# Attention: chunk outputs turned by plain transposes, halves added by VectorE, inverse of the sums applied in the output block by GpSimd

## The reference, cut to what matters

```python
p = jax.nn.softmax(jnp.where(mask, s, -jnp.inf), axis=-1)      # fox heads; the memory heads without a mask
o = jnp.einsum('bhqk,bkhd->bqhd', p.astype(v.dtype), v)
...
y = jnp.concatenate([_normalize(y_conv), _normalize(y_fox), _normalize(y_mem)], axis=-1)   # RMS norm of each group
y = (y * out_norm_g).astype(y_conv.dtype)
return y @ w_out
```

## Time and profile before

| | |
|---|---|
| median of 3 runs | 2729.73 us (2722.56 to 2731.79) |
| span of the profiled execution | 2721.6 us |
| PE, DVE, POOL, ACT busy | 96%, 72%, 64%, 43% |
| attend, 560 to 1116 us: PE, POOL, DVE, ACT busy | 519.9, 536.7, 475.7, 427.0 us of 556 |

### The profile page before, as it was taken

How to read it: one execution, slowest core, us unless ns; L and a number is a source line. 1 busy time by engine, 2 the same in 40 slices (tenths; PEclk the granted TensorE clock), 3 DMA queues, 4 the chain that set the end, 5 groups by cost and what they waited for, 6 DMA issues and landing times. The chain is left out here.

```text
span 2721.6 us, 42356 instructions
## 1 busy us (share of the span) xinstructions
PE 2611.8 (96%) x14722; PEld 2358.1 (87%) x14722; DVE 1950.3 (72%) x2561; ACT 1168.6 (43%) x2053; POOL 1733.3 (64%) x1004
## 2 busy tenths in 40 slices
PE   8999999889999998899999999999999999999998
PEld 7999899877777777777799998999999997888887
DVE  5366687588888888666587888787887784454564
ACT  4222321377777778533353334333433332232343
POOL 3487688489999999565656776677656660222232
PEclk9999999999999999999999999999999999999999
DMA  6587899666667676775635343534345536755564
GB/s 207 176 258 251 272 295 308 174 175 177 174 187 192 181 191 185 232 247 188 201 105 174 115 132 114 174 114 132 115 117 152 157 104 202 245 171 179 182 227 139
DMA packets 470965, 498.20 MB, mean 183 GB/s; under 512 B 172171, under 2 KB 359558, under 8 KB 469722
## 3 DMA queue, kind: packets, MB, share of 16 engines
q1 hardware_dynamic: 449970, 470.00, 57.5%
q10 hardware_dynamic: 20496, 24.45, 2.6%
q0 software_dynamic: 288, 1.05, 0.1%
HBM read 398.11 MB, written 94.16 MB: 181 GB/s over the span
## 5 line engine op out<-in xcount | busy, mean ns | idle before, releaser
L2792 PE MATMUL ps_gate_up<-h_hi,w_hi 128*128 128x344 f32 (+1 forms) x1584 | 510.3, 322 | 12.3 <-DVE h_lo L2658 12.1
L2793 PE MATMUL ps_gate_up<-h_lo,w_hi 128*128 128x344 f32 (+1 forms) x1584 | 508.2, 321 | 0.0
L2794 PE MATMUL ps_gate_up<-h_hi,w_lo 128*128 128x344 f32 (+1 forms) x1584 | 507.3, 320 | 0.0
L2792 PEld LDWEIGHTS ps_gate_up<-h_hi,w_hi 128*128 128x128 f32 x1584 | 299.8, 189 | 15.1 <-DVE h_lo L2658 14.0
L2794 PEld LDWEIGHTS ps_gate_up<-h_hi,w_lo 128*128 128x128 f32 x1584 | 300.3, 190 | 0.0
L2793 PEld LDWEIGHTS ps_gate_up<-h_lo,w_hi 128*128 128x128 f32 x1584 | 300.1, 189 | 0.0
L881 PE MATMUL ps_proj<-w_hi,h_lo 128*128 128x428 f32 (+1 forms) x800 | 283.3, 354 | 0.0
L1599 DVE TENSOR_TENSOR split_halves<-ps_turned,split_halves 128x512 fp32r<-128x512 f32 (+1 forms) x352 | 210.5, 614 | 63.0 <-ACT split_halves L1486 60.5
L2986 POOL TENSOR_TENSOR stock<-common 128x512 f32<-128x512 f32 x55 | 87.0, 1593 | 261.1 <-DMA common<-in_w_down 260.9
L2517 POOL TENSOR_TENSOR stock<-common 128x512 f32<-128x512 f32 x64 | 103.5, 1616 | 232.3 <-DVE w_lo L2643 232.3
L3188 PE MATMUL ps_down<-wd_hi,split_halves 128*128 128x512 f32 x616 | 241.4, 392 | 6.0 <-DVE wd_lo L3096 5.9
(11 more groups left out here) (396 smaller groups left out, 7326.9 us busy)
## 6 DMA issues: line engine op xcount, KB each, us to landing
stock<-in_cache_k SPq DMA_DIRECT2D x192, 256.0 KB, 3.4
common<-in_cache_v SPq DMA_DIRECT2D x172, 256.0 KB, 3.1
stock<-act_combined SPq DMA_DIRECT2D x56, 704.0 KB, 4.2
common<-in_w_gate SPq DMA_DIRECT2D x33, 1024.0 KB, 5.4
common<-in_w_up SPq DMA_DIRECT2D x33, 1024.0 KB, 5.9
common<-in_w_down SPq DMA_DIRECT2D x44, 512.0 KB, 5.9
page_v<-in_cache_v SPq DMA_DIRECT2D x84, 256.0 KB, 3.0
common<-in_w_in SPq DMA_DIRECT2D x44, 428.0 KB, 4.7
```

Source lines behind the costliest of these rows:

```text
L2792: pe.matmul(acc, a_hi, h_hi[:, d, :], start=d == 0, stop=False)
L2793: pe.matmul(acc, a_hi, h_lo[:, d, :], start=False, stop=False)
L2794: mm = pe.matmul(acc, a_lo, h_hi[:, d, :], start=False, stop=d == H - 1)
```

## The change

The output of a chunk is turned by four plain transposes of 128x128 against the unit matrix instead of the four products with `fold`. The two halves then lie side by side in PSUM and VectorE adds them with a `tensor_reduce` over an innermost axis of two. Nothing is divided in `attend` any more. ScalarE accumulates the row sums straight into a kept buffer `inverse` of 12 heads by 16 tiles, which VectorE inverts in place once per head. The rows that are stored are not normalised. Tile 0 is multiplied in `attend` by VectorE (`first_scaled`, once for the fox heads, once for the memory heads), and ScalarE's squares wait for that. Tiles 1 to 15 are multiplied in `combine` by GpSimd (`scale_heads`), which waits for the landing of the tile; ScalarE's squares wait for GpSimd. Some small buffers move to other storage.

```diff
@@ attend, TensorE
                         for r in range(QCH):
-                            mm = pe.matmul(out[:, r * HD:(r + 1) * HD], a.o_t[:, k % 2, r * P:(r + 1) * P], c.fold[:], start=True, stop=True)
-                        mm.then_inc(s.o_ready, 1)
+                            turned = pe.transpose(out[:, r * P:(r + 1) * P], a.o_t[:, k % 2, r * P:(r + 1) * P], c.ident[:])
+                        turned.then_inc(s.o_ready, 1)
@@ attend, VectorE
+                def first_scaled(h0, h1):
+
+                    own = y_first[:, CW + h0 * HD:CW + h1 * HD].rearrange("p (h d) -> p h d", d=HD)
+                    dve.tensor_tensor(own, own, a.inverse[:, h0:h1, 0:1].to_broadcast([P, h1 - h0, HD]), ALU.mult).then_inc(s.first_scaled, 1)
...
-                        dve.reciprocal(a.inv[:, part], a.sums[:, parity, part]).then_inc(s.inverted, 1)
-                        dve.wait_ge(s.inverted, k + 1)
+                        k = chunk_index[u.head, u.ch]
+                        halves = ps_t[:, bank_of["fold", k], :].rearrange("p (r s d) -> p r d s", r=QCH, s=2)
                         dve.wait_ge(s.o_ready, k + 1)
                         if u.head:
                             dve.wait_ge(stored[u.ch], 16 * u.head)
-                        dve.tensor_tensor(a.o_out[:, u.ch, :, :], ps_t[:, bank_of["fold", k], 0:QCH * HD].rearrange("p (r d) -> p r d", d=HD),
-                                          a.inv[:, part].unsqueeze(2).to_broadcast([P, QCH, HD]), ALU.mult).then_inc(s.o_out, 1)
+                        dve.tensor_reduce(a.o_out[:, u.ch, :, :], halves, AX.X, ALU.add).then_inc(s.o_out, 1)
+                        if u.ch == NT // QCH - 1:
+                            dve.wait_ge(s.probs, exp_index[u.head, NT - 1] + 1)
+                            dve.reciprocal(a.inverse[:, u.head, :], a.inverse[:, u.head, :]).then_inc(s.inverted, 1)
+                    if n == last_chunk + 4:
+                        dve.wait_ge(s.fox_ahead, 16)
+                        dve.wait_ge(s.inverted, FH)
+                        first_scaled(0, FH)
+                dve.wait_ge(s.mem_ahead, 16)
+                dve.wait_ge(s.inverted, FH + MH)
+                first_scaled(FH, FH + MH)
@@ attend, ScalarE
-                        act.wait_ge(s.fox_ahead, 16)
+                        act.wait_ge(s.first_scaled, 1)
...
-                act.wait_ge(s.mem_ahead, 16)
+                act.wait_ge(s.first_scaled, 2)
                 first_square(2)
@@ combine, GpSimd
+                def scale_heads(k):
+
+                    own = y[k % 3][:, CW:].rearrange("p (h d) -> p h d", d=HD)
+                    pool.wait_ge(y_in[k % 3], y_landed(k))
+                    pool.tensor_tensor(own, own, c.inverse[:, :, k:k + 1].to_broadcast([P, FH + MH, HD]), ALU.mult).then_inc(s.y_scaled, 1)
...
+                scale_heads(1)
                 for k in range(N):
                     if k:
                         root(k)
+                    if 1 < k + 1 < NT:
+                        scale_heads(k + 1)
                     if CONVS <= k + 1 < NT:
                         conv(k + 1)
@@ combine, ScalarE
-                        act.wait_ge(y_in[k % 3], y_landed(k))
+                        act.wait_ge(s.y_scaled, k)
```

More of the change, by code:

```diff
@@ L128, in finish_constants @@
     dve.tensor_copy(c.causal_r[:], causal[:])
-    dve.tensor_copy(c.fold[0:HD, :], c.ident[0:HD, 0:HD])
-    dve.tensor_copy(c.fold[HD:P, :], c.ident[HD:P, HD:P])
     for k in range(P // PAGES):
@@ L1139, in attend @@
                  "q0 q1 k0 k1 v0 v1 decay page0 page1 page2 weighed halved added "
-                 "raised conv_w_in conv_in0 conv_in1 conv_step conved gain_ahead fox_ahead mem_ahead first_squares first_var first_root first_normed")
+                 "raised conv_w_in conv_in0 conv_in1 conv_step conved gain_ahead fox_ahead mem_ahead first_scaled first_squares first_var first_root first_normed")
         with stage(nc, names) as (block, s):
@@ L1467, in exps @@
                         act.activation(out, src, ACT.Exp, scale=-1.0, bias=a.low[:, parity, i:i + 1],
-                                       accum_out=a.sums[:, parity, i:i + 1]).then_inc(s.probs, 1)
+                                       accum_out=a.inverse[:, piece.head, i:i + 1]).then_inc(s.probs, 1)
                 for n in range(SLOTS_ALL):
@@ L1602, in _ @@
                     if u:
-                        k, parity = chunk_index[u.head, u.ch], u.head % 2
-                        part = slice(QCH * u.ch, QCH * u.ch + QCH)
-                        dve.reciprocal(a.inv[:, part], a.sums[:, parity, part]).then_inc(s.inverted, 1)
-                        dve.wait_ge(s.inverted, k + 1)
+                        k = chunk_index[u.head, u.ch]
+                        halves = ps_t[:, bank_of["fold", k], :].rearrange("p (r s d) -> p r d s", r=QCH, s=2)
                         dve.wait_ge(s.o_ready, k + 1)
@@ L1690, in combine @@
         ss, rstd = sb("sum_squares", [P, N, 3]), sb("rstd", [P, N, 3])
-        sm, ones_8 = sb("sums", [P, NS + NM]), sb("ones_8", [P, DB])
-        small, wide = sb("small", [P, 2, FH]), sb("wide", [P, DB, FH])
+        listed, at = c.pages[:].bitcast(F32), 0
+        sm, at = listed[:, at:at + NS + NM], at + NS + NM
+        ones_8, at = listed[:, at:at + DB], at + DB
+        small, at = listed[:, at:at + 2 * FH].rearrange("p (a h) -> p a h", a=2), at + 2 * FH
+        wide = listed[:, at:at + DB * FH].rearrange("p (b h) -> p b h", b=DB)
         h_out = sb("h_turned", [P, 2, DT, P])
@@ L3231, in decoder_step @@
                   page_before=y_first[:, 0:P], seq_of_page=early_sb("seq_of_page", [P, 2, DB]),
-                  fold=early_sb("fold", [P, HD]), ones=early_sb("ones", [P, 1]),
-                  pages=early_sb("pages", [1, DB * PAGES], I32), page_index=early_sb("page_index", [P, 2], U32),
+                  inverse=early_sb("inverse_sums", [P, FH + MH, NT]), ones=early_sb("ones", [P, 1]),
+                  pages=early_sb("pages", [P, DB * PAGES], I32), page_index=early_sb("page_index", [P, 2], U32),
                   gathered=whole.enter_context(nc.semaphore("gathered")), kept=whole.enter_context(nc.semaphore("kept")),
@@ L3268, in decoder_step @@
             project_all(nc, c, io, scratch, dec, shared, common, key_pages, last_page, fox_head(0), y_first)
+            probs = sb("probs", [P, 2, QCH, SEQ])
+            past_rows = probs[:, 1, 0, SEQ - (QCH - 1) * P:]
             a = group(q=shared.q, k=shared.k, v=shared.v, neg_cum=shared.decay, k_st=sb("k_stacked", [P, SEQ], F32R),
                       q_hi=sb("q_hi", [P, SEQ], F32R), q_lo=sb("q_lo", [P, SEQ], F32R), v_st=sb("v_stacked", [P, 2, NT, P], F32R),
-                      probs=sb("probs", [P, 2, QCH, SEQ]), p_hi=halves[:, 0:2 * D].rearrange("p (k n) -> p k n", k=4), p_lo=halves[:, 2 * D:4 * D].rearrange("p (k n) -> p k n", k=4),
-                      o_t=shared.o_t, kept=shared.o_t.rearrange("p b (e c) -> p (b e) c", e=2), o_out=sb("o_out", [P, QCH, QCH, HD]), low=sb("low", [P, 2, NT]),
-                      first_low=sb("first_low", [P, NT]), sums=sb("row_sums", [P, 2, NT]), inv=sb("inverse", [P, NT]),
+                      probs=probs, low=past_rows[:, 0:2 * NT].rearrange("p (a t) -> p a t", a=2), first_low=past_rows[:, 2 * NT:3 * NT], p_hi=halves[:, 0:2 * D].rearrange("p (k n) -> p k n", k=4), p_lo=halves[:, 2 * D:4 * D].rearrange("p (k n) -> p k n", k=4),
+                      o_t=shared.o_t, kept=shared.o_t.rearrange("p b (e c) -> p (b e) c", e=2), o_out=sb("o_out", [P, QCH, QCH, HD]), inverse=c.inverse,
                       page_v=[first[:, k].rearrange("p d n -> p (d n)").rearrange("p (j n) -> p j n", j=4) for k in range(2)] + [sb("page_v", [P, 4, FW])[:]], page_sum=shared.sums, row=shared.row)
```

2 lines of the change are left out of this document (1 added, 1 removed).

## The result

The changed kernel takes 2735.60 us (median of 20 runs, 2730.19 to 2741.63); the kernel before, run beside it on the same chip, 2726.55 (20 runs, 2720.45 to 2735.14). The ratio is 1.0034, with a 95% interval of 1.0026 to 1.0043: 9 us slower. The prediction had +8.0 us, at the border of what can be told from no change, and 2738 in a range of 2720 to 2748.

The account below looks back on a forecast made before the run. GpSimd was taken to bound attend and a ring of VectorE, ScalarE and GpSimd work most of combine. Attend -1.2 and combine +9.2 gave +8.0 us, added to the median: 2738 us, range 2720 to 2748.

Parts of the forecast that it names:

- S: Combine: time of one `scale_heads` op on GpSimd, 768 elements with a repeated operand, 1.46 us, bounds 1.36 and 1.87.
- The reduction: Attend: VectorE's new reduction of 512 elements from PSUM takes 0.68 us, or about 1.1 by a strided row.
- The ring: Combine's gapless chain of VectorE, ScalarE and GpSimd ops per tile, a period of 13.74 us, was to grow by 0.73.
- GpSimd's waits: Attend: faster slots shorten GpSimd's waits for pages behind the first page's, -1.7 us, bounds 0 and 8.4.
- x_root(0) behind scale(3): Start of combine: x_root(0) queues behind the scaling of late-landing tile 3 on GpSimd and runs 3.4 us late.
- PE's 0.9 for the weights: Start of combine: the sixth weight block reaches PE later, about 0.9 us, covered by the 3.4 us lateness beside it.
- Tiles 8 to 11 cost nothing: Combine: these periods lie where PE has more work and sets the pace, so the longer period adds nothing.
- (a): Rival: PE's gain in attend reaches the end, -21 + 9.2, about 2718 us; chance 0.12.
- (b): Rival: the scaling is hidden in combine, leaving +1 to +4, about 2731 us; chance 0.15.
- (c): Rival: scaling op at 1.87 us and attend's reduction at 1.1, giving 2742 to 2747 us; chance 0.18.
- (d): Rival: attend's transposes are no cheaper than the products; time as forecast plus at most 1.7 us; chance 0.55 together with the forecast.
- The 0.5 us of `first_scaled`: End of attend: tile 0's memory-part scaling between landing and ScalarE's squares adds 0.5 us; its fox part adds nothing.

Follow-up runs that it names:

- `no_scale`: The changed kernel without the scaling in combine, so tiles 1 to 15 stay undivided: 2729.13 us, ratio 1.0001 to the kernel before.
- `scale_late`: The changed kernel with GpSimd's scaling of tile k+1 moved behind x_root(k-2) in its queue: 2731.42 us, ratio 1.0013 to the kernel before.
- `scale_only`: The kernel before plus only GpSimd's scaling op in combine, multiplying by ones, at the changed kernel's place: 2739.96 us, ratio 1.0045.
- `rows_before`: The kernel before with eight of GpSimd's additions in attend given to PE as second accumulating products: 2733.39 us, ratio 1.0024.
- `rows_late`: `scale_late` with eight of GpSimd's additions in attend given to PE: 2728.61 us, ratio 1.0009 to the kernel before.
- `dve_scale`: The changed kernel with the scaling of tiles 1 to 15 in combine done by VectorE instead of GpSimd: 2731.28 us, ratio 1.0016.
- `ordered`: `dve_scale` with eight attend additions on PE, tile 0's fox scaling later, and, in combine, GpSimd's convolution waiting for VectorE's normalising, x_root earlier: 2719.96 us.

## Why the prediction was right, and where it was not

**What was right.** That a kernel 96% busy on PE would not gain from less work on PE in attend: `no_scale` and the stage lengths show it (-0.3 us, forecast -1.2). S: 1.50 us for 1.46. The reduction: 681 ns for 0.68. The Trainium skill ("VectorE: DVE Perf Modes", table of modes) gives `tensor_reduce` one element a cycle, which at the 0.96 GHz of the same page is 1.04 ns. The traces agree for PSUM: 681 ns for 512 elements and 1214 for 1024 are 533 ns apart, 1.04 ns for each of the 512. The reason given for 0.68, transposed reads of PSUM elsewhere, was not one: VectorE's large reads of PSUM in the kernel before (L1599, L2008, L2025) run along neighbouring elements, so the strided read was first measured by this run. The ring: VectorE's ops end behind GpSimd's, and the period grew by 0.76 (0.73). Combine as a whole came to +9.3 for +9.2, but that agreement is in part luck, as the terms below show.

**GpSimd's waits (forecast -1.7).** They fell from 21.5 to 19.1 us, 0.9 of that before the stage begins; the third, which was to vanish, went from 1.71 to 0.72. GpSimd's last convolution op ends 576.0 us behind its first page multiplication (577.0 before), and from there to combine are 5.9 us (5.2 before), where `first_scaled` stands. So the stage shows -1.0 + 0.7 = -0.3 for -1.7 + 0.5 = -1.2. All of this lies within the 2.6 us by which attend differs between kernels with this same chain (580.2 to 582.8), so the step is neither shown nor refuted.

**x_root(0) behind scale(3) (forecast 3.4 us).** This step failed. scale(3) began at 1150.94, 23.7 us behind the stage's start, where the prediction had tile 3 landing 25.9 behind it (1148.3 - 1122.4). So it ended in time, and x_root(0) ran right behind its own input. It was late by 1.8 for another reason, which the prediction had not looked at: scale(2), beside VectorE's weight blocks, makes the squares of tile 2 late, with them root(2) and VectorE's normalising of tile 2, behind which the residual of tile 0 stands, whose squares x_root(0) needs. PE's 0.9 for the weights came as forecast (16.0 - 15.1) and lay beside it. `scale_late`, where x_root(0) stands ahead of scale(3), keeps just these 1.8 us. The wait of PE before its turn of tile 3, forecast at 3 us or more, is 1.8. The landing of tile 3 does matter, but by another way than the one forecast: in `scale_only`, where it came 0.9 us earlier, the scaling met VectorE's normalising of tile 2 and root(3) was 3.1 us late.

**Tiles 8 to 11 cost nothing (forecast).** Also wrong. From root 8 to root 10 it grew by another 1.6 us; only from 10 to 12 it did not. I had put the start of PE's own stretch at the product of tile 6 and did not look at the periods there: before, root 8 follows root 7 by 98.9 - 85.2 = 13.7 us, which is the ring's pace, not PE's. So ten periods carry the 0.75, not eight, 7.5 us for 5.8. The two errors, -1.6 and +1.7, cancelled: the sum was better than its terms.

**The rivals.** (a), PE's gain reaches the end, fell in the changed kernel, but it was nearer than its chance says: PE stood 5 us behind GpSimd, and "PE has no say in attend's end" holds only as long as PE gets faster. `rows_before` shows the other side: slower slots bring the pages later, and GpSimd waits. And of the 21 us, even free of GpSimd, 6.5 arrived. (b), hidden scaling, is what `scale_late` does, by place; GpSimd is idle even more than the 30% given there, 73 of 190 us from 1150 to 1340 before. (c) fell with the two measured durations. (d) fell: 29.4 us of records for 48.7.

**The 0.5 us of `first_scaled`.** On the memory part as forecast: 0.42 us between landing and squares. The fox part was costed at nothing, with PE's lead as cover; where the cover is gone (`rows_late`) it is 4.0 us of PE's wait.

## What to carry to other kernels

Work moved to an idle engine is paid for by its place in that engine's queue: the same 1.5 us op cost 0.75 us a period ahead of the convolution and nothing behind x_root. Where VectorE and GpSimd both read SBUF, put the short ops of the one where the other is idle, even if it has to wait for that: 1.7 us of idle time put in on purpose took 3.6 us out of the chain and, with x_root moved ahead, made the period 1.3 us shorter than in `dve_scale`, down to where PE became the bound. And when an engine at 96% is not the bound, find out how near it stands behind the one that is, by making the other lighter, before giving it any work.

## What the runs showed of the hardware

- Three VectorE ops with two SBUF inputs on 256, 512 and 256 elements take 1.54 us with GpSimd idle, 5.17 to 5.19 beside GpSimd's convolution, and 5.95 when a 1.50 us op stands ahead of it. A GpSimd op of 0.19 us takes 0.84 when it starts during a VectorE op of 0.94. That VectorE op takes 2.4 us in `ordered`, where it runs beside GpSimd's convolution. The Trainium skill ("SBUF — State Buffer", section "Who interferes with whom") says that an op of VectorE with two SBUF inputs and an op of GpSimd that reads SBUF exclude each other for the whole instruction, whichever comes first. The traces agree in both directions.
- GpSimd, two inputs, one of them a repeated column: 1.50 us for 768 elements in combine, 1.90 for 1024 and 3.62 for 2048 in attend. A plain one takes 1.84 for 768.
- A VectorE reduction over pairs that lie 64 elements apart in PSUM takes 681 ns for 512 elements, no more than a row of 1214 ns for 1024 neighbouring elements leads one to expect. The strided reduction of 2048 from SBUF takes 4123 ns.
